# Merge weights kept as bf16 in DRAM, scale before shift in the first norm, and finer pieces between attention steps

## What is computed

```python
mod = silu(c) @ w_mod + b_mod                      # 12288 values: 6 vectors of 2048
sh_a, sc_a, g_a, sh_f, sc_f, g_f = split(mod, 6)
h = rms_norm(x, norm_a) * (1.0 + sc_a) + sh_a
q_a, k_a, v_a, q_r, k_r, v_r, g_r, gate_a, gate_r = split(h @ w_in)
o_a = attention(rope(rms_norm(q_a)), rope(rms_norm(k_a)) + cached keys, v_a + cached values)
o_r = bidirectional chunkwise retention(q_r, k_r, v_r), normed, * silu(g_r)
merged = sigmoid(gate_a) * (o_a @ w_ba) + sigmoid(gate_r) * (o_r @ w_br)
x = x + g_a * (merged @ w_out)
h = rms_norm(x, norm_f) * (1.0 + sc_f) + sh_f
x = x + g_f * ((silu(h @ w_g) * (h @ w_u)) @ w_d)
y = rms_norm(x, final_norm)
```

## Time and profile before

| what | value |
|---|---|
| time, median of 3 runs | 3709.5 us (3707.75 to 3755.76) |
| the profiled execution's own time | 3722.3 us |
| its span on the slowest core | 3721.2 us |
| spans of the 8 cores | 3685.6 to 3721.2 us |
| TensorE busy | 3377.6 us (91%) |
| VectorE, ScalarE, GpSimd busy | 30%, 20%, 6% |
| bytes read from DRAM, written | 902.53 MB, 41.98 MB |

### The profile page before, as it was taken

One profiled execution on the slowest core, in us unless ns is written; L12 is line 12 of the kernel. 1 busy time (PEld: TensorE's weight loads), 2 busy tenths in 40 slices (PEclk: granted clock), 3 DMA queues, 4 the chain that ended last, 5 costly groups with the idle time before them and its releaser, 6 DMA issues.

```text
span 3721.2 us, 52224 instructions; the slowest of 8 cores (3685.6 to 3721.2 us)
## 1 busy us (share of the span) xinstructions
PE 3377.6 (91%) x19697; PEld 1721.0 (46%) x19697; DVE 1116.0 (30%) x2685; ACT 726.1 (20%) x1454; POOL 219.7 (6%) x417
## 2 busy tenths in 40 slices
PE   2588888888999998989997998999999999999998
PEld 1244555664566553434443443444444444444443
DVE  1354454324666664112222113111112100120004
ACT  3222455642222220001111011110001000000001
POOL 0000000000000000000000000000000000000000
PEclk9798999999999999989998999999999999999999
DMA  9866544342232237989999996999899998999985
GB/s 201 164 125 108 93 91 96 61 86 43 55 69 60 49 70 154 188 162 202 181 170 189 194 162 147 201 169 167 146 151 213 168 173 147 149 223 169 173 146 129
DMA packets 99925, 525.29 MB, mean 141 GB/s; under 512 B 11808, under 2 KB 35296, under 8 KB 41056
## 3 DMA queue, kind: packets, MB, share of 16 engines
q0 software_dynamic: 61392, 422.60, 67.4%
q1 hardware_dynamic: 38288, 99.37, 8.3%
HBM read 902.53 MB, written 41.98 MB: 254 GB/s over the span
## 4 chain that ended last, share of the span: by engine, by line
PE 80%; DMA 11%; DVE 4%; issue 2%; ACT 2%; another core or an unknown queue 1%; DVEq 0%; SPq 0%; ACTq 0%; POOL 0%; POOLq 0%
PE pbk L296 78%; DMA sb_wsl<-w_mod 3%; DMA sb_xsl<-x 2%; DMA sb_wsl<-w_in 2%; DMA sb_wsl<-w_g 1%; PE pbk L299 1%; DMA sb_wsl<-w_u 1%; DMA sb_wsl<-w_br 1%; ACT sb_pT L303 1%; DVE sb_nw L314 1%; DMA sb_wsl<-w_out 1%; DMA sb_oaB<-oas 0%; DVE sb_ont L311 0%; DVE sb_ut L314 0%
## 5 line engine op out<-in xcount | busy, mean ns | idle before, releaser
L296 PE MATMUL pbk<-sb_hT,sb_wsl 128*128 128x512 bf16 x7296 | 1609.3, 381 | 32.6 <-DMA sb_wsl<-w_g 17.0
L296 PEld LDWEIGHTS pbk<-sb_hT,sb_wsl 128*128 128x128 bf16 x7296 | 715.2, 98 | 889.0 <-issue 60.2
L296 PE MATMUL pbk<-sb_wsl,sb_hT 128*128 128x256 bf16 (+1 forms) x2688 | 482.5, 329 | 25.7 <-ACT sb_hT L303 10.2
L296 PE MATMUL pbk<-sb_wsl,sb_hid 128*128 128x512 bf16 x2112 | 456.6, 379 | 1.5 <-DMA sb_wsl<-w_d 1.5
L296 PEld LDWEIGHTS pbk<-sb_wsl,sb_hT 128*128 128x128 bf16 x2688 | 259.8, 100 | 160.7 <-issue 59.5
L314 DVE TENSOR_TENSOR sb_hid<-pbk,sb_su 128x512 bf16<-128x512 f32 x132 | 91.1, 692 | 797.0 <-PE pbk L296 797.0
L296 PEld LDWEIGHTS pbk<-sb_wsl,sb_hid 128*128 128x128 bf16 x2112 | 206.5, 98 | 251.1 <-issue 2.4
L303 ACT ACTIVATE sb_pT<-pbk 128x512 bf16<-128x512 f32 x416 | 224.9, 603 | 114.9 <-PE pbk L296 113.7
L303 ACT ACTIVATE sb_su<-pbk 128x512 bf16<-128x512 f32 x132 | 78.8, 597 | 792.8 <-PE pbk L296 792.8
L314 DVE TENSOR_TENSOR sb_tB<-pbk,sb_bcg 128x512 f32<-128x512 f32 x96 | 66.2, 689 | 484.9 <-PE pbk L296 484.9
L296 PE MATMUL pbk<-sb_or,sb_wsl 128*128 128x512 bf16 x768 | 173.9, 385 | 31.6 <-DMA sb_or<-ors 27.0
(11 more groups left out here) (140 smaller groups left out, 2052.2 us busy)
## 6 DMA issues: line engine op xcount, KB each, us to landing
sb_wsl<-w_in POOLq DMA_DIRECT2D x84, 1024.0 KB, 13.5
sb_wsl<-w_g POOLq DMA_DIRECT2D x66, 1024.0 KB, 23.0
sb_wsl<-w_u POOLq DMA_DIRECT2D x66, 1024.0 KB, 22.9
sb_wsl<-w_d POOLq DMA_DIRECT2D x60, 1024.0 KB, 9.7
sb_wsl<-w_mod POOLq DMA_DIRECT2D x48, 1024.0 KB, 10.7
sb_wsl<-w_ba POOLq DMA_DIRECT2D x24, 1024.0 KB, 14.6
sb_wsl<-w_br POOLq DMA_DIRECT2D x24, 1024.0 KB, 13.9
sb_wsl<-w_out POOLq DMA_DIRECT2D x24, 1024.0 KB, 12.2
```

What stands on the lines that cost most here:

```text
L296: K.op("pe", lambda: nc.tensor.matmul(out, lhsT=lhsT, rhs=rhs, start=start, stop=stop), reads, writes)
```

## The change

- A DRAM tensor `wc` holds bf16 copies of the 40 weight tiles of the merge stage. `precast` issues one DMA from DRAM to DRAM that casts one tile; 21 are issued within the query projections beside attention, 2 beside its last group, the rest at the head projections of retention. The merge stage loads from `wc` (`mload`) instead of casting the float32 tile in each of its three blocks.
- In `modq` the 8 scale tiles come before the 8 shift tiles. `scale` writes scaled copies `hS` of the sample tokens; the keys of 4 tiles and the values of 8 are projected from them. `shift` then adds the shift's part: the shift, broadcast over 128 columns (`shB`), is multiplied with the key and value weights into the same banks, and for the values into bank 4, from which `v_add` adds it. `modulate` still completes `hT`. Key and value weights are loaded earlier.
- The scaling of normed keys (tiles 0 to 7) and of the first queries moves from VectorE to ScalarE (`onact`), in four operations per tile.
- A modulation step is cut into four pieces (`mod_parts`); in the first query projection it rotates over slots 4, 7 and 8. Projection pieces beside attention have 2 matmuls, `ft` counts 1.6 for a modulation step. `v_gen` beside the last group has pieces of 4 instead of 8.
- In block 0 of the merge the second gate R comes before the first `branch`; `held_last` runs one chain step later, and the chain is cut at 7 pieces instead of 5.

The diff, without its unchanged lines:

```diff
+    wc_d = nc.dram_tensor("wc", [40, 128, 4096], BF16, kind="Internal").ap()
...
-        def wload(parts, s=None):
+        def wload(parts, s=None, reads=()):
...
-                DMA("pool", wsl[s][:, off:off + ne], src, wsem[s], [], [wbuf[s]])
+                DMA("pool", wsl[s][:, off:off + ne], src, wsem[s], list(reads), [wbuf[s]])
...
+        mkeys = [k_ for cg in range(8) for k_ in (("w_in", win_idx(9216 + 256 * cg)), ("w_in", win_idx(11264 + 256 * cg)), ("w_ba", cg), ("w_br", cg))]
+        mkeys += [("w_out", i) for i in range(8)]
+        mcb = {k_: Buf() for k_ in mkeys}
+        mcsem, mcrot = [K.dsem(f"mc{i}") for i in range(8)], [Buf() for _ in range(8)]
+        mcn = [0]
...
+        def precast(n=1):
+            for _ in range(n):
+                i = mcn[0]
+                if i < len(mkeys):
+                    mcn[0] += 1
+                    DMA("pool", wc_d[i, :, :], wt(*mkeys[i]), mcsem[i % 8], [], [mcb[mkeys[i]], mcrot[i % 8]])
...
+        def mload(nm, i):
+            return wload([(wc_d[mkeys.index((nm, i)), :, :], 0)], None, [mcb[(nm, i)]])
...
-        modq = [c + 8 * i for c in range(8) for i in range(2)] + list(range(16, 48))
...
-        def mod_step(bank, s=None):
+        modq = list(range(8, 16)) + list(range(8)) + list(range(16, 48))
...
+        def mod_parts(bank, s=None, extra=0):
...
+            precast(extra)
...
+                    if k % 8 == 7 and (j, k) != (1, 15):
+                        yield
...
+        def mod_step(bank, s=None, extra=0):
+            for _ in mod_parts(bank, s, extra):
+                pass
...
-        def modulate(c):
...
+        hS = [r(f"hS{k}", 16 + 2 * k if k < 8 else 76 + 2 * k, [128, 1024], BF16) for k in range(16)]
+        hSb = [Buf() for _ in range(16)]
+        shB = r("shB", 90, [128, 8, 128], BF16)
+        shBb = [Buf() for _ in range(4)]
...
+        def scale(c):
...
+            for k in (2 * c, 2 * c + 1):
+                hs, hbs = hT[:, 0:2, k, :], [hTb[t][k] for t in range(8)]
+                dst = hS[k][:].rearrange("p (b t) -> p b t", b=2)
+                if k % 2 == 0:
+                    ACT(dst, hs, AF.Identity, hbs + [mb], [hSb[k]], scale=col(gsa, k, 0))
+                else:
+                    TS(dst, hs, col(gsa, k, 0), None, ALU.mult, None, hbs + [mb], [hSb[k]])
...
+        def modulate(c):
...
-            return (4, 5, 6, 0, 1)[n % 5] if n < 10 else (4, 5, 6)[n % 3]
+            return (4, 5, 6, 0, 1)[n % 5] if n < 8 else (4, 5, 6)[n % 3]
...
+            if t == 5:
+                kpair = wpair("w_in", win_idx(2048), 7)
+        vpair = wpair("w_in", win_idx(2560), 0)
...
-        K.inherit(flat(kTb) + vb, xb[0:4])
-        K.inherit(utb + [t2b], xnb[0:2])
...
-        kpair = wpair("w_in", win_idx(2048), 7)
+        vst = r("vst", 0, [128, 8, 512], F32)
+        vstb = [Buf() for _ in range(8)]
+        K.inherit(vstb, xb[0:2])
+        K.inherit(hSb[0:8], xb[2:4])
+        K.inherit(hSb[8:16], xnb[0:2])
...
-        for kt in range(16):
-            MEMSET(vall[:, kt, :, 128:129], 1.0, [vb[kt]])
...
-        KO = 6
...
-        def kproj_mm(t, bk, bkb, k0, nk):
-            acc(bk, bkb, 512, lambda k: htile(t, k), lambda k: kpair[k // 8][0][:, k % 8, :], nk,
-                lambda k: [hTb[t][k], kpair[k // 8][1]], k0=k0, ktot=16)
...
-        vpair = None
...
-        def mods_to(n):
-            while 48 - len(modq) < n:
-                mod_step((pbk[6 + len(modq) % 2], pbb[6 + len(modq) % 2]), start_slot())
...
-        mods_to(2)
-        modulate(0)
+        KO = 4
...
-            if c < 7:
-                mods_to(2 * c + 4)
-                modulate(c + 1)
-            if c == 6:
-                vpair = wpair("w_in", win_idx(2560), 0)
+            scale(c)
+            if c == 1:
...
-                    x_load(t, [hTb[0][2 * c]])
+                    x_load(t, [hSb[2]])
...
-                kproj_mm(t, pbk[t], pbb[t], 2 * c, 2)
+                acc(pbk[t], pbb[t], 512, lambda k: hS[k][:, t * 128:(t + 1) * 128], lambda k: kpair[k // 8][0][:, k % 8, :], 2,
+                    lambda k: [hSb[k], kpair[k // 8][1]], k0=2 * c, ktot=17)
...
-        held = set()
+        held = {4}
...
-        def z_scale(i, t, kout):
+        def z_scale(i, t, kout, onact):
...
+            if onact:
+                for g in range(4):
+                    gs = slice(g * 128, (g + 1) * 128)
+                    c_ = (i % 2) * 4 + g
+                    ACT(qb[i % 4][:, gs], ut[i % 4][:, gs], AF.Identity, [utb[i % 4], rstb[p2]], [qbb[i % 4]], scale=rst[:, p2, c_:c_ + 1])
+                return
...
-        def proj_gen(pair, tiles, tab, tabb, ni, dstT, dstTb, banks, kout=False, pre=0, mods=(), step=4):
+        def proj_gen(pair, tiles, tab, tabb, ni, dstT, dstTb, banks, kout=False, pre=0, mods=(), mcast=0, step=4, onact=False, mslots=(4,)):
...
-                        if k0 + 2 * step == 16 and scaled is not None and t % 2 == 1:
+                        if k0 == 8 and step < 16 and scaled is not None and t % 2 == 1:
...
-                        if k0 + 2 * step == 16 and ready is not None and t % 2 == 0:
+                        if k0 == 8 and step < 16 and ready is not None and t % 2 == 0:
...
-                        z_scale(ready[0] + a, ready[1] + a, kout)
+                        z_scale(ready[0] + a, ready[1] + a, kout, onact)
...
-                    mod_step(pool_bank(banks), 4)
-                    yield 0.8
+                    mbank = pool_bank(banks, True)
+                    for _ in mod_parts(mbank, mslots[len(modq) % len(mslots)], mcast):
+                        yield 0.4
+                    release(mbank[0])
+                    yield 0.4
...
-                z_scale(ready[0] + a, ready[1] + a, kout)
+                z_scale(ready[0] + a, ready[1] + a, kout, onact)
...
-        brot[0] = 6
-        kg = proj_gen(kpair, range(8), ktab, ktabb, 1, kT, kTb, ALLB, pre=KO, step=16)
...
+        FREEB = [5, 6, 7]
...
+        def v_raw(t):
+            bk, bkb = pool_bank(FREEB)
+            acc(bk, bkb, 512, lambda k: hS[k][:, t * 128:(t + 1) * 128], lambda k: vpair[k // 8][0][:, k % 8, :], 16,
+                lambda k: [hSb[k], vpair[k // 8][1]])
+            if t % 2 == 0:
+                CPA(vst[:, t, :], bk[:], [bkb], [vstb[t]])
+            else:
+                CPV(vst[:, t, :], bk[:], [bkb], [vstb[t]])
...
+        def v_add(t):
+            TT(vall[:, t, :, 0:128], vst[:, t, :].rearrange("p (g d) -> p g d", g=4), pbk[4][:].rearrange("p (g d) -> p g d", g=4), ALU.add,
+               [vstb[t], pbb[4]], [vb[t]])
...
+        def shift(c):
...
+            mod_step(pool_bank(FREEB), start_slot())
+            s2 = slice(2 * (c % 4), 2 * (c % 4) + 2)
+            CPV(shB[:, s2, :], modt[:, 2 * c:2 * c + 2, 0].unsqueeze(2).to_broadcast([128, 2, 128]), [mb], [shBb[c % 4]])
+            for k in (2 * c, 2 * c + 1):
+                for t in range(KO):
+                    MM(pbk[t][:], shB[:, k % 8, :], kpair[k // 8][0][:, k % 8, :], False, k == 15, [shBb[c % 4], kpair[k // 8][1]], [pbb[t]])
+                MM(pbk[4][:], shB[:, k % 8, :], vpair[k // 8][0][:, k % 8, :], k == 0, k == 15, [shBb[c % 4], vpair[k // 8][1]], [pbb[4]])
+            modulate(c)
...
-            src = bk[:].rearrange("p (g d) -> p g d", g=4)
-            if t % 2 == 0 or t >= 8:
-                CPA(vall[:, t, :, 0:128], src, [bkb], [vb[t]])
-            else:
-                CPV(vall[:, t, :, 0:128], src, [bkb], [vb[t]])
-            if t >= 8:
-                u, ub = nvst[t % 4], nvb[t % 4]
-                CPV(u[:], bk[:], [bkb], [ub])
-                DMA("sp", nv_d[(t - 8) * 128:(t - 7) * 128, :], u[:], utsem[t % 4], [ub], [], is_out=True)
+            CPA(vall[:, t, :, 0:128], bk[:].rearrange("p (g d) -> p g d", g=4), [bkb], [vb[t]])
+            u, ub = nvst[t % 4], nvb[t % 4]
+            CPA(u[:], bk[:], [bkb], [ub])
+            DMA("sp", nv_d[(t - 8) * 128:(t - 7) * 128, :], u[:], utsem[t % 4], [ub], [], is_out=True)
...
-        K.inherit(nvb, [wbuf[6]])
...
-        kdone = False
...
-            for _ in range(3):
-                if not kdone and next(kg, "done") == "done":
-                    kdone = True
-            v_tile(t)
-            if t == 1:
+            v_raw(t)
+            if t % 2 == 1:
+                shift(t // 2)
+            if t == 2:
...
-            if t == 3:
+            if t == 4:
...
-                mod_step(pool_bank(ALLB), 4)
-            if t == 4:
...
-            if t == 6:
-                for tt in (10, 11):
-                    x_trans(tt)
-                for k in range(16):
-                    modulate_p(k)
-        if not kdone:
-            run(kg)
+        for tt in (10, 11):
+            x_trans(tt)
+        for k in range(8):
+            modulate_p(k)
+        for c in range(4, 8):
+            shift(c)
+            for k in (2 * c, 2 * c + 1):
+                modulate_p(k)
+        K.inherit(nvb, [wbuf[6]])
+        K.inherit(vb, hSb[0:8])
```

(49 more changed lines are left out.)

## The result

The changed kernel takes 3767 us (3760.4, 3765.3, 3767.9 and 3769.2) where the kernel before takes 3709.5: ratio 1.0154, 95% interval 1.0129 to 1.0178. Executions in which a die had a lower clock throughout (here one of 4351.5 us) are left out everywhere. The forecast was 3619 us (0.976); the time lies outside the range, on the other side. It is slower by less than 2%, but the interval keeps clear of 1: the 2% that I took for the limit of such a measurement was too coarse.

A forecast was written before the change was run, and what follows sets the result against it. Bound by TensorE (80% of the wait chain, DMAs 11%), through its stalls and lower clock. 64 - 3 + 4 + 14 + 6 + 6 = 91 us off 3722, then 12.8 lower for the median: 3619 us, range 3580 to 3675.

The forecast's parts named there:

- Part 2: Forty DRAM-to-DRAM casts beside attention and retention, 6.2 us each: 3 us lost, bounds 0 and 15.
- Part 3: Start, up to the first query projection: 145 us against 149, 4 won; bounds 12 lost and 15 won.
- Part 4: First query projection: three w_mod slots end the waits, ScalarE relieves VectorE; 14 us won, bounds 5 and 18.
- Part 1: Merge stage: bf16 loads and the new order shorten TensorE's stalls for DMAs; 64 us won.
- Part 5: Attention: finer pieces shorten waits for the exponentials; 6 us won, bounds -5 and 25.
- the w_in waits: Start of attention: two waits from POOL standing behind w_mod loads go; 6 us won, bounds 2 and 8.
- seven: 43 us on top of 58, so it fits: Seven casts per 125 us attention group add 43 us of DMA time to 58, within the group.
- My sign for trouble: Casts landing later than 12 us after their issue would show the forecast wrong.
- The price c: DMA time of one DRAM-to-DRAM cast: taken as 6.2 us, between 3.3 and 12.4.
- Rival (d): Attention: dear casts eat up the 91 us at 14 us each; at 20 each, 3835 us; chance 0.06.
- my bound of 12 lost: Worst case for the start: slow clock for all shifts and ScalarE late, 12 us lost.
- All 29.5 us: Merge block 2: the whole stall for the retention outputs' load goes, 29.5 us won, lower bound 5.

The follow-up runs named there:

- 24-tile kernel: Kernel before plus three w_mod slots (VectorE scaling), the merge's new order and 24 tiles copied from retention's third head on; first score at 311.6 us.
- start-as-before kernel: Changed kernel with the old first norm modulation, key and value projections and w_mod order; ratio 1.0046 against the kernel before, 3717.6 to 3728.9 us.

## Why the prediction failed

The forecast was 91 us won and the measurement is 57 lost, 148 apart. In means over the cores 59 of it are Part 2, 48 are Parts 3 and 4, 20 are Part 1 and some 12 are Part 5 and the w_in waits; the rest is that the time is the slowest core's and not the mean.

**Part 2 is the step that failed**: "seven: 43 us on top of 58, so it fits", 3 us lost. It cost 62, all ahead of retention; in retention itself the copies cost nothing, as I had it (534.5 against 533.9). Room in the sum of DMA time isn't the condition; the landing time of whatever has a deadline is. I had named one such DMA (w_mod, bounds 0 and 15) and missed the other: the stores behind two buffers, to which the question "who waits when this lands late" was never put. And I took the stretch in which conversions run from the code instead of from POOL's timeline, whose 28 us of standing still ahead of a burst shows how far it runs ahead. My sign for trouble was right: landings over 12 us; they are 13 to 20.

The price c itself: 29 conversions in core 1's attention added 0.86 x 512.9 - 0.46 x 501.5 = 210 us of DMA time, 7.3 each. (The 9.6 in my expectation for 40 tiles counted 23 conversions instead of 29.) That is between my 6.2 and the 9.8 us that I estimated from the 214 GB/s of the Trainium skill (DMA: Bandwidth & Descriptors, Latency and other measured facts). Rival (d), the nearest to what happened, put the whole loss on c and asked for 14 to turn the sign. With 7 the conversions cost 62 us where the copies bring 34, because waits begin before the engines are full, at a share of 0.86; the rest of the loss is the start's.

**Part 3**, forecast as 4 us won, cost 22 up to the first query projection on core 1 (171.3 us from the first key matmul, against 149.2; I had 145). The counts were right, 384 + 80 matmuls. Groups of TensorE's instructions in that stretch (busy us, mean ns; idle before, releasers):

```profile
L297 PE MATMUL pbk<-sb_wsl,sb_hT 128*128 128x512 bf16 x192 | 44.9, 395 | 0.0
L297 PE MATMUL pbk<-sb_wsl,sb_hS 128*128 128x512 bf16 x192 | 44.4, 392 | 10.4 <-ACT sb_hS L304 9.6 <-ACT sb_hT L324 0.8
L297 PE MATMUL pbk<-sb_wsl,sb_shB 128*128 128x512 bf16 x80 | 23.5, 452 | 14.9 <-DVE sb_shB L321 14.9
...
L300 PE MATMUL pbk<-sb_identb,sb_qb 128*128 128x128 bf16 x48 | 5.3, 247 | 22.9 <-ACT sb_qb L304 18.5 <-DVE sb_qb L315 4.3
```

Too small were the slow clock (44.9 + 44.4 + 23.5 = 113 us busy for 464 x 0.216 = 100, so 13 where I had 5), the shifts' waits (14.9 for 6) and the wait for scaled tiles (22.9 for 14): 26 us together, which is 171 instead of 145 and past my bound of 12 lost. The operations were the ones I had named; their waits were mis-sized.

**Part 4** was two edits with opposite signs. Three slots took the w_mod waits away and, alone, bring the first score 13 us forward (311.6 in the 24-tile kernel against 324.8; I had 14). Scaling on ScalarE, the only other difference ahead of attention in the start-as-before kernel but for one conversion some 5 us ahead of the first score, gives all of it back: 327.0 (326.0 on the cores with the usual clock). I had counted it as relief for VectorE (39.8 us busy of 70.8, so no bound) and not as a longer chain: eight operations of 0.39 us are 3.1 us for a pair where VectorE needs 1.3.

**Part 5**, forecast as 6 us won, brought nothing: waits for the exponentials fell from 34.9 to between 22 and 25 in the kernel without conversions, and attention stayed at 474.4 (474.5 before). That a wait ended by one engine's pace was shortened, and not the pace, is how I read it; no run shows it.

**Part 1**, forecast as 64 us won, was right in kind: of the stalls for DMAs ahead of w_g one is left, for w_out, 9.5 us where I left some 8, and one of 8.1 for VectorE's `sb_orS` is new. On core 1 the merge went from 898.3 to 841.4, 57 us; but core 1 was the worst of eight (874 to 898), and the mean fell by 44, 10 of them by the new order alone. The page shows the slowest core, and a stall read there is in part what made it the slowest. "All 29.5 us" for the retention outputs held: they land in 9.3 to 12.6 us by core instead of 22.9 to 56.7, and no stall for them is left. The Trainium skill's turn-taking by packet (same page, Queues, rings and completion order) agrees in direction, as would any other way of sharing. The same rule, turned round, spoke against Part 2: there small rows had to share with more traffic. I weighed it only where it helped.

What stays open: whether the stores land late because of how engines share packets, or because memory is slower beside copies from DRAM to DRAM; and whether the spacing of the conversions counts or only how many there are. No run separates them.

## What to carry to other kernels

Before moving traffic into a stage that "has room", list each transfer there that something waits for, with its buffers and its landing time now, and ask what happens at three times that; small stores behind two buffers come first. Find where a DMA without waits is really issued from the issuing engine's timeline, not from its place in the code. And convert only what relieves the full stage: 24 of 40 tiles, late and with the new order, shortened the merge by 45 us and lengthened no stage, where 40 late ones shortened it by 48 and lengthened retention by 97.

## What was unexpected of the hardware

The DMA time of one and the same conversion grew with the company. On core 2, in 520 us of retention, the share was 0.30 without conversions, 0.39 with 10 (the change: 4.7 us each), 0.60 with 20 (7.8) and 0.88 with 33 (9.1). That "busy" also counts packets that wait would explain it, but no run shows it. A store of 128 KB went from 4.3 us to 14.2, and to as much as 28 on the chain, at a DMA share of 0.86. So the DMA time of one transfer, read at one level of traffic, isn't a price that can be multiplied.
